# Gates in DRAM by expert group first: where the 512-byte runs of a transposing round trip stand

## The reference, cut to what matters

```python
def blk(tb):                                   # one block of tokens
    q = (tb @ wq).reshape(TOK_BLOCK, PEER_HEADS, 2, PEER_DK)
    s = jnp.einsum('thpd,hpkd->thpk', q, keys)
    sv, si = lax.top_k(s, PEER_TOPK)
    ...
    eid = (i1 * PEER_NKEYS + i2)               # expert numbers
    g = jax.nn.softmax(fv, axis=-1)            # their gates
    hid = jax.nn.gelu(jnp.einsum('td,ted->te', tb, u_tab[eid]), approximate=False)
    return jnp.einsum('te,ted->td', g * hid, v_tab[eid])
```

## Time and profile before

| | us |
|---|---|
| median of 3 runs | 2293.75 |
| lowest, highest | 2291.79, 2295.91 |
| the profiled execution | 2290.24 |
| its span | 2288.4 |
| PE busy | 2195.8 |
| DVE busy | 1674.1 |
| ACT busy | 925.1 |
| POOL busy | 389.8 |

### The profile page before, as it was taken

How to read it: one execution, slowest core, us unless ns; L and a number is a source line. 1 busy time by engine, 2 the same in 40 slices (tenths; PEclk the granted TensorE clock), 3 DMA queues, 4 the chain that set the end, 5 groups by cost and what they waited for, 6 DMA issues and landing times.

```text
span 2288.4 us, 38652 instructions
## 1 busy us (share of the span) xinstructions
PE 2195.8 (96%) x14886; PEld 1936.8 (85%) x14886; DVE 1674.1 (73%) x3098; ACT 925.1 (40%) x1080; POOL 389.8 (17%) x337
## 2 busy tenths in 40 slices
PE   7899999779989999999999999999999999999996
PEld 1598889448969989999988888889888898989996
DVE  3279777434457699878887787887878888877686
ACT  1333232453343228644434434344343343444444
POOL 1053000300000008101122222221212322111000
PEclk9999999889999999999999999999999999999998
DMA  9978767967653545788899999999999999988863
GB/s 401 381 268 283 283 225 258 386 259 289 233 183 114 163 150 228 268 303 289 293 339 346 341 368 352 355 370 326 364 365 342 360 354 364 343 311 303 284 206 128
DMA packets 158263, 673.87 MB, mean 294 GB/s; under 512 B 17328, under 2 KB 18736, under 8 KB 135056
## 3 DMA queue, kind: packets, MB, share of 16 engines
q1 hardware_dynamic: 122112, 444.65, 55.1%
q0 software_dynamic: 33648, 219.49, 24.8%
q10 hardware_dynamic: 2336, 7.39, 0.9%
HBM read 649.51 MB, written 21.95 MB: 293 GB/s over the span
## 4 chain that ended last, share of the span: by engine, by line
PE 82%; DVE 8%; DMA 7%; ACT 2%; issue 1%; SPq 0%; DVEq 0%; POOL 0%; ACTq 0%
PE vb L1643 16%; PE zb L1628 14%; PE vb L1645 7%; PE zb L1630 6%; PE zb L546 6%; PE zb L548 5%; PE zb L547 5%; PE vb L1677 3%; PE vb L1667 3%; PE vb L1266 3%; DMA ada_first<-in_w_ada 3%; PE vb L1608 2%; DMA raw<-in_v 2%; DVE lo L486 1%; PE zb L1584 1%; PE vb L1642 1%
## 5 line engine op out<-in xcount | busy, mean ns | idle before, releaser
L477 ACT ACTIVATE hi<-raw 128x1024 fp32r<-128x1024 f32 x624 | 659.5, 1059 | 971.5 <-PE vb L1643 300.9
L486 DVE TENSOR_TENSOR lo<-raw,hi 128x1024 fp32r<-128x1024 f32 x624 | 766.0, 1231 | 265.7 <-ACT hi L477 261.0
L1628 PE MATMUL zb<-act_hl,hi 128*128 128x416 f32 x1792 | 556.5, 368 | 0.0
L1643 PE MATMUL vb<-w_rest,hi 128*128 128x416 f32 x1536 | 495.3, 367 | 0.0
L1630 PE MATMUL zb<-act_hl,lo 128*128 128x208 f32 x1680 | 435.4, 259 | 0.0
L1628 PEld LDWEIGHTS zb<-act_hl,hi 128*128 128x128 f32 x1792 | 334.9, 188 | 36.0 <-issue 27.7
L1645 PE MATMUL vb<-w_rest,lo 128*128 128x208 f32 x1280 | 329.7, 258 | 0.0
L1630 PEld LDWEIGHTS zb<-act_hl,lo 128*128 128x128 f32 x1680 | 320.4, 191 | 5.1
L1643 PEld LDWEIGHTS vb<-w_rest,hi 128*128 128x128 f32 x1536 | 288.5, 188 | 1.4
L546 PE MATMUL zb<-act_hl,hi 128*128 128x288 f32 x960 | 287.1, 299 | 0.4 <-DVEq L1918 0.4
L547 PE MATMUL zb<-act_hl,hi 128*128 128x288 f32 x960 | 282.6, 294 | 0.0
(11 more groups left out here) (299 smaller groups left out, 2758.8 us busy)
## 6 DMA issues: line engine op xcount, KB each, us to landing
raw<-in_v SPq DMA_DIRECT2D x256, 512.0 KB, 6.4
raw<-in_u SPq DMA_DIRECT2D x224, 512.0 KB, 6.5
raw<-in_w_in SPq DMA_DIRECT2D x80, 512.0 KB, 9.1
ada_first<-in_w_ada SPq DMA_DIRECT2D x64, 512.0 KB, 8.7
ada_mid<-in_w_ada SPq DMA_DIRECT2D x64, 512.0 KB, 5.3
ada_in<-in_w_ada SPq DMA_DIRECT2D x32, 512.0 KB, 8.7
raw<-in_w_out SPq DMA_DIRECT2D x32, 512.0 KB, 5.6
ada_last<-in_w_ada SPq DMA_DIRECT2D x32, 512.0 KB, 6.8
```

The costliest lines, as they stand in the source:

```text
L477: act.activation(hi[s][:, :], raw[s][:, :], ACT.Copy).then_inc(hi_ready, 1)
L486: dve.tensor_tensor(lo[s][:, :], raw[s][:, :], hi[s][:, :].bitcast(F32), ALU.subtract) \
L1628: last = pe.matmul(zb[:, bank, 0:2 * ND], w_h, act_hl[:, k, :, 0:ND], start=(k == 0), stop=(k == KC - 1))
L1643: last = pe.matmul(vb[:, bank, 0:2 * ND], v_h, w[:, e % 2, :, :], start=(e == 0), stop=(e == GI - 1))
```

## The change

The DRAM tensor gates has its axes in another order. Before, a block of tokens comes first: [13 blocks, 128 partitions, 128 i2 x 16 tokens]. After, the group of experts comes first: [16 groups, 128 partitions, 13 blocks, 8 i2 x 16 tokens]. The bytes stored and loaded are the same, and so are the tiles in SBUF.

- A store of a block (1 MB): before one contiguous run of 8192 bytes per partition, 128 runs; after 16 runs of 512 bytes per partition, 2048 runs, 6656 bytes apart from partition to partition and 851968 bytes from group to group.
- A load of a group (832 KB): before 13 runs of 512 bytes per partition, 1664 runs; after one run of 6656 bytes per partition, 128 runs, which also follow each other without a gap.

No instruction is added, removed or moved on any engine: PE, DVE and ACT have the same instructions in the same order, and on POOL 13 stores and 14 loads stand where they stood, with other access patterns. The waits are the same.

```diff
-    gates_d = nc.dram_tensor("gates", [TBLKS, P, NK * TB], F32).ap()
+    gates_d = nc.dram_tensor("gates", [NG, P, TBLKS, GI * TB], F32).ap()
...
             def load_gates(g):
 
-                src = gates_d[:, :, GI * TB * g:GI * TB * (g + 1)].rearrange("b p x -> p b x")
-                pool.dma_start(Gb[g % 2][:, :, :], src).then_inc(gates_in[g % 2], 16)
+                pool.dma_start(Gb[g % 2][:, :, :], gates_d[g]).then_inc(gates_in[g % 2], 16)
 
             def keep_block(blk):
 
                 pool.wait_ge(g_copied, 2 * blk + 4)
-                pool.dma_start(gates_d[blk], stage[blk % 2][:, :, :].rearrange("p i t -> p (i t)")) \
+                pool.dma_start(gates_d[:, :, blk, :].rearrange("g p x -> p g x"),
+                               stage[blk % 2][:, :, :].rearrange("p (g i) t -> p g (i t)", i=GI)) \
                     .then_inc(g2_out[blk % 2], 16)
```

## The result

The changed kernel has a median of 2306.13 us (2303.09 to 2309.41, 5 runs); its time is 1.0052 times that of the kernel before, 95% interval 1.0036 to 1.0068: slower by 0.5%, 12 us. Of five new executions of the kernel before that were taken for the comparison, one lasted 7239 us and is left out of the ratio; nothing on record explains it. The forecast was 2294 us with a range of 2288 to 2304, so the time lies above the range, between the prices of rival 1 (2304 us, chance 0.11) and rival 2 (2311 us, chance 0.05).

A forecast was written before the change was run, and what follows sets the result against it. PE was taken to bound the kernel, with PE and DVE pacing the gates stage. Terms 0.3 + 0.95 - 1.0 = +0.25 us gave 2290.5 us for the profiled execution and a median of 2294 us, range 2288 to 2304.

The forecast's parts named there:

- rival 1: Gates stage, ACT's wait for a staging buffer: slow short writes land after 7.3 us, +10 us, 2304 us; chance 0.11.
- rival 2: Gates stage: POOL's store issue ends only after DVE's comparisons, tiles 1.4 us late 12 times, 17 us, 2311 us; chance 0.05.
- What bounds the kernel: PE at 96% of the span; PE and DVE pace the gates stage; the expert loop has 7.7 us idle to win.
- The issue: POOL's issue of a store in the gates stage: 1.3 us, 0.7 more than now.
- The bytes: Engine time of a store's short runs into DRAM: 0.5 us more than the present 2.5 us.
- The landing: Store from issue to landing: 4.1 + 0.7 + 0.5 = 5.3 us, bounds 4.7 to 7.6.
- The rhythm of the two buffers: Alternating staging buffers in the gates stage: a landing of 5.3 us costs 0; blocks stretch only above 6.3 us.
- the spare of POOL's tiles: POOL's one-hot tiles behind a store's issue: 1.1 us spare before PE starts, against 0.7 more, so cost 0.
- The first store: Gates stage: its later landing delays ACT's evacuation and PE's group 6, +0.3 us, bounds 0 to 2.6.
- The last store on buffer 1: End of gates stage: DVE waits for it, delaying PE's value products, +0.95 us, bounds +0.3 to +3.3.
- The loads: Expert loop: cheaper gate loads leave engines to weight loads PE awaits, -1.0 us, bounds 0 to -4.4.
- The sum: First store, last store and loads: 0.3 + 0.95 - 1.0 = +0.25 us, forecast 2294 us.

The follow-up runs named there:

- the doubled stores: Changed kernel with stores of blocks 0 to 11 issued by SP, each made twice, second copy into another DRAM tensor; ratio 1.0069 to the kernel before.
- two issues: Kernel before, old layout, each store made as two stores of half a block on POOL; ratio 0.9996 to the kernel before.
- the swapped order: Changed kernel, but in token groups behind a store DVE builds one2 first and its six tiles after; ratio 0.9999 to the kernel before.

## Why the prediction was wrong, point by point

- **What bounds the kernel, and that only the gates stage and the loop can matter**: right.
- **The issue**: 1.3 us forecast, 1.21 measured. **The bytes**: 0.5 us more forecast, 0.2 measured (2.7 against 2.5 us). **The landing**: 5.3 forecast, 5.3 measured, which is partly luck: its two terms measured 0.6 + 0.2 of the 1.2 us, and 0.3 us is in neither. The Trainium skill's rule that was set against the row, full rate from 512 bytes ("DMA: Bandwidth & Descriptors", "Specifications"), came nearer than the row of the load, which had been taken beside other traffic: the engines' time for one store is 9% higher (45.4% against 41.5% of 6 us), not half.
- **The rhythm of the two buffers**: right, both that 5.3 us costs nothing by itself and where it begins to cost (the doubled stores).
- **The step that failed** is the spare of POOL's tiles: "Spare: 1.1 us, against 0.7 more (1.0 at most). Cost 0; if the issue took over 1.7 us, each excess would reach PE 12 times". The issue took less than forecast, and it cost 11 us. The sum behind the 1.1 us moved POOL's tiles by 0.6 us and kept their duration of 0.85 to 0.9 us. But those durations were taken where the tiles hardly met DVE's tensor_tensor: the second one began at 871.0, and the tensor_tensor at 871.76. It is this lead of 0.75 us, and not the distance to PE's start at 873.07, that was the spare, and not all of it: a longer issue of 0.53 us (two issues) leaves the tile free, one of 0.62 to 0.65 us does not. The trace of before had one tile that was held, the third of all, before any store: it began at 855.17, 0.2 us before a tensor_tensor, and is the maximum in this line:

```profile
L762 POOL TENSOR_SCALAR one<-consts,i1T,gT x52: 845/894/1916, 853.4 to 922.9; 128x128 f32<-128x128 f32 x52
```

  Once held, POOL runs behind and meets both tensor_tensors of a block: 0.8 and 1.0 us, which is the 5.19 us for four tiles, and with the issue 6.40 us per block. Against 5.46 us the first four blocks lose 2.2 us, the next six 5.6 and the last, with the tile of 3.9 us, 3.0: 10.8 us.
- **Rival 2** put the trouble at the right engine and between the right two instruction streams, and its price of 17 us was near, by luck: it let DVE's tensor_scalar hold up the issue. The issue kept to 1161 to 1252 ns, and the one from 901.93 to 903.14 lies beside DVE's six comparisons (901.49 to 903.88). It was DVE's tensor_tensor that held up the tiles. The rival also misread where the issue of 869.46 begins in the kernel before. DVE is not idle there:

```profile
869.03 1.21 DVE L2218 TENSOR_TENSOR one<-consts,i2T 128x1024 f32<-128x1024 f32 x1
```

  The issue of 0.59 us lay inside this tensor_tensor and was not held. The Trainium skill ("SBUF — State Buffer", section "Who interferes with whom"), cited there for tensor_scalar, says in the same list that a VectorE instruction with two SBUF inputs contends with a GpSimd instruction that reads SBUF. The traces agree with that sentence: 1.64 and 1.85 us for a tile beside the tensor_tensor, 0.86 clear of it, at most 1.30 with the tensor_tensor replaced. It bore on this change and was not weighed. No run here separates the second SBUF operand from the length of the instruction (1.21 us) as the reason.
- **The first store**: +0.3 forecast; the trace shows no such cost. The evacuation that needs its buffer begins at 871.53 and waits for PE, not for the store. ACT's two waits for stores (2.50 us up to 896.08, 1.85 up to 915.38; landings of 6.9 and 7.0 us) stand in later blocks, and those blocks take 6.40 us like their neighbours.
- **The last store on buffer 1**: the mechanism was right, the size was not. DVE waited 8.4 us instead of 2.4. Where POOL keeps its pace the term holds: DVE waits 2.2 us with the swapped order. In the changed kernel the store is issued late, behind the tile of 3.9 us, at 935.97, when SP's loads of v have begun (934.41); it lands after 8.0 us, and that these loads share the engines with it is the likely reason, not one that a run isolates. From that issue to the first value product (952.83) it is 16.9 us, before 13.3: 3.5 us more, a second consequence of the same cause.
- **The loads**: -1.0 forecast, -1 measured twice, within the noise; PE's idle time from 950 to 2200 fell by 2.7 us in the profiled execution, but from the first value product to the end it is 1351.1 us before and 1351.5 after, so this pair of executions shows no gain. POOL's issue fell to 0.567 us and gained nothing, as forecast.
- **The sum**: 10.8 (rhythm) + 3.5 (tail) make 14.3 of the 15.9 us between the two spans; 1.2 us lie ahead of the first store, where nothing was changed, and are the difference of two executions. In the prediction's rival 1 the block of 11.9 / 2 us is 5.95 and not 5.97, which takes 0.2 us off its price and changes nothing else. The median of the runs moved by less, 12 us: the profiled execution of before was a quick one.

## What to carry to other kernels

An engine's spare time depends on place: before counting on it, look at what the shifted instructions will lie beside. Ask of each neighbour on VectorE (DVE) whether it is a tensor_tensor with two operands in SBUF, because in this kernel the duration of a GpSimd (POOL) instruction held only for the neighbours that it had. When a rhythm is tight, a small shift can decide between nothing and ten microseconds (here leads of 0.5 and 0.2 us), so a forecast that leans on a small margin in a repeated stage should carry a larger chance for the cliff. And a transfer's issue can matter more than its bytes: try another engine's queue, or another order beside it, before blaming the layout.

## What the runs showed of the hardware that was not expected

- A POOL tensor_scalar of 128x128 takes 0.78 to 0.96 us clear of DVE's tensor_tensor (1.21 us); where DVE builds one2 from tensor_scalars instead, 0.86 to 1.30 us. Started 0.5 us before one, it is not held, though it overlaps by 0.35 us (0.87 us). Started inside one, it ends 0.66 to 0.85 us after that one's end (the two of 3.9 us, which meet three in a row, aside), so the hold-up depends on where it starts: 1.15 us for the tile of 872.58 in the kernel before, 1.64 and 1.85 us in the changed kernel.
- Started 0.15 to 0.28 us before one, either can lose. In the changed kernel five tiles took 1.87 to 2.00 us and the tensor_tensor its 1.21; three others (870.10, 875.80, 878.84) took 0.83 to 0.90 us and the tensor_tensor 1.31 to 1.39. The leads overlap, so what decides is open. No tile in these traces starts between 0.28 and 0.50 us before one.
- The span of POOL for issuing a store grows far less than its runs: 0.59 us for 128, 1.21 for 2048; on SP's queue the same two stores take 0.32 and 0.36 us.
- 2048 runs of 512 bytes into DRAM took 2.7 us of the 16 engines, 128 runs of 8 KB 2.5 us.
